# Reordering the first eleven projections behind the join of two transformer blocks, and folding two norms into one token factor

## The reference, cut to what matters

```python
# end of first_block
x = x + swiglu_ffn(rms_norm(x, norm_ffn), w_gate_up, w_down)
x = rms_norm(x, final_norm)                  # norm 2 of the kernel
# start of second_block
x = x + ab_mixer(rms_norm_2(x, ab_norm), ab_w_in, ...)   # norm 3 of the kernel

def ab_mixer(h, ...):
    p = h @ w_in
    qk, va, oa, gates, uv = split(p)         # 1024, 512, 512, 16, 1024 columns
    qk = silu(centred_dwconv(qk, conv_w))    # 5 taps along the tokens
    ...                                      # mLSTM over q, k, va with the gates
    u, vb = split(gelu(uv))
    vb = rms_norm_2(vb by groups)            # then mixed over the tokens by ws
    return concatenate([ha * sigmoid(oa), u * sp]) @ w_out
```

## Time and profile before

| | us |
|---|---|
| median of 3 runs | 895.58 |
| lowest and highest run | 895.4, 896.25 |
| the profiled execution, its own time | 894.72 |
| its span, first to last instruction | 893.0 |
| TensorE busy | 866.3 |
| VectorE busy | 529.4 |
| ScalarE busy | 431.3 |

### The profile page before, as it was taken

How to read it: one execution, slowest core, us unless ns; L and a number is a source line. 1 busy time by engine, 2 the same in 40 slices (tenths; PEclk the granted TensorE clock), 3 DMA queues, 4 the chain that set the end, 5 groups by cost and what they waited for, 6 DMA issues and landing times.

```text
span 893.0 us, 14170 instructions
## 1 busy us (share of the span) xinstructions
PE 866.3 (97%) x5809; PEld 782.9 (88%) x5809; DVE 529.4 (59%) x558; ACT 431.3 (48%) x574; POOL 46.9 (5%) x104
## 2 busy tenths in 40 slices
PE   4999999999999799999999999999999999999997
PEld 4987899999999699888999999989967899999996
DVE  5656554544544669588665555557676765555553
ACT  6366353443444457752654444436565374444441
POOL 4000000000000200211000000003000000000000
PEclk9999999999999899999999999999999999999999
DMA  9821245555546564335675555443611566555511
GB/s 312 302 95 56 86 164 194 185 188 188 188 146 233 185 194 142 142 95 189 184 250 185 186 185 190 142 159 104 216 48 48 189 226 200 187 188 188 188 47 48
DMA packets 98538, 148.20 MB, mean 166 GB/s; under 512 B 4019, under 2 KB 81907, under 8 KB 98499
## 3 DMA queue, kind: packets, MB, share of 16 engines
q1 hardware_dynamic: 97202, 143.11, 48.5%
q0 software_dynamic: 1264, 4.52, 1.7%
q10 hardware_dynamic: 32, 0.02, 0.0%
HBM read 146.57 MB, written 1.05 MB: 165 GB/s over the span
## 4 chain that ended last, share of the span: by engine, by line
PE 93%; DVE 3%; ACT 2%; POOL 1%; DMA 1%; issue 1%; DVEq 0%; POOLq 0%; ACTq 0%
PE bank L1712 28%; PE bank L1713 27%; PE bank L1714 27%; PE bank L1786 1%; PE bank L2285 1%; PE bank L2308 1%; DMA gain<-in_norm_mix 1%; PE bank L2270 1%; PE bank L2264 1%; PE bank L1874 1%; ACT x_norm L646 1%; PE bank L1886 1%; PE bank L1873 1%; PE bank L2039 0%; PE bank L2011 0%
## 5 line engine op out<-in xcount | busy, mean ns | idle before, releaser
L1081 DVE TENSOR_TENSOR w_lo<-w_raw,w_hi 128x2048 fp32r<-128x2048 f32 (+1 forms) x130 | 292.0, 2254 | 151.2 <-ACT w_hi L617 150.9
L1712 PE MATMUL bank<-xT_hi,w_hi 128*128 128x256 f32 x1068 | 304.1, 285 | 0.0
L1714 PE MATMUL bank<-xT_hi,w_lo 128*128 128x256 f32 x1068 | 302.7, 283 | 0.0
L1713 PE MATMUL bank<-xT_lo,w_hi 128*128 128x256 f32 x1068 | 302.7, 283 | 0.0
L617 ACT ACTIVATE w_hi<-w_raw 128x2048 fp32r<-128x2048 f32 (+1 forms) x130 | 243.0, 1878 | 93.2 <-PE bank L1714 83.1
L1712 PEld LDWEIGHTS bank<-xT_hi,w_hi 128*128 128x128 f32 x1068 | 204.3, 191 | 4.2 <-issue 2.4
L1713 PEld LDWEIGHTS bank<-xT_lo,w_hi 128*128 128x128 f32 x1068 | 204.3, 191 | 1.9 <-issue 0.2
L1714 PEld LDWEIGHTS bank<-xT_hi,w_lo 128*128 128x128 f32 x1068 | 204.3, 191 | 0.2
L1712 PE MATMUL bank<-w_hi,ff_hi 128*128 128x512 f32 x344 | 134.6, 391 | 0.0
L1713 PE MATMUL bank<-w_lo,ff_hi 128*128 128x512 f32 x344 | 134.5, 391 | 0.0
L1714 PE MATMUL bank<-w_hi,ff_lo 128*128 128x512 f32 x344 | 134.0, 390 | 0.0
(11 more groups left out here) (234 smaller groups left out, 681.9 us busy)
## 6 DMA issues: line engine op xcount, KB each, us to landing
w_raw<-in_ffn_w SPq DMA_DIRECT2D x64, 1024.0 KB, 5.3
w_raw<-in_ffn_w_gate_up SPq DMA_DIRECT2D x22, 1024.0 KB, 5.1
w_raw<-in_ab_w_in SPq DMA_DIRECT2D x12, 1024.0 KB, 5.3
w_raw<-in_ffn_w_down SPq DMA_DIRECT2D x11, 1024.0 KB, 4.8
w_raw<-in_swa_w_in SPq DMA_DIRECT2D x5, 1024.0 KB, 10.8
w_raw<-in_swa_w_out SPq DMA_DIRECT2D x4, 1024.0 KB, 8.0
w_raw<-in_ab_w_out SPq DMA_DIRECT2D x4, 1024.0 KB, 5.6
w_raw<-in_c_w_out SPq DMA_DIRECT2D x4, 1024.0 KB, 5.2
```

Source lines behind the costliest of these rows:

```text
L1081: dve.tensor_tensor(view(w_lo, ch), view(w_raw, ch), view(w_hi, ch).bitcast(F32), ALU.subtract).then_inc(S["lo_done"], 1)
L1712: pe.matmul(out, sh, mh, start=first, stop=False)
L1713: pe.matmul(out, sh, ml, start=False, stop=False)
L1714: return pe.matmul(out, sl, mh, start=False, stop=last)
```

## The change

- `normalise` no longer runs at the join. VectorE multiplies both gains once (`joined_gains`) and writes `x_norm` = x times both gains (`both_gained`), which is transposed without any token factor. Tile 0's transposes are issued inside the last `down`, tile 1's inside the first visit.
- The raw transposes are split into `uT_hi` and `uT_lo` (`plain_high`, `plain_low`). These two live in `w_hi` and `w_lo` of the slot `up`, which holds no chunk until the seventh of the phase: the ring has three slots until then.
- The two `va` chunks and the two `vb` chunks come first, token-major, with these operands (`plain_visit`). The token factor of both norms together, `ab_rc`, enters as ScalarE's `scale` when the result is read (`mixing_values`, `spatial_values`). The gates come fifth, q and k sixth to ninth, then `u` and `oa` as before.
- For the feature-major chunks the factor must be along the free axis. GpSimd spreads `ab_rc` to 128 columns (`ab_rb`), TensorE transposes it into bank 4, VectorE copies it to `ab_R`, multiplies the transposes in banks 0 to 3 by it in place (`scaled`), and ScalarE and VectorE split that into `xT_hi` and `xT_lo`.
- The second norm's sum of squares is taken over x times the first gain (`first_gained`, `ab_y`); the first token factor is put into `x_res` later by ScalarE, four 128x512 copies with a scale, between the two gelus of `vb`.
- GpSimd makes `ab_r2` and `ab_rc` in small steps, two each token tile; its memsets of the padding wait for the fourth chunk. The gain loads `next_gain(2)` and `next_gain(3)` are behind them.
- VectorE's squares of `vb` and their sum stand before the first `conv` instead of behind the last.
- `decay_rows(0)` waits for the gates' raw row, chunk index 9 for both gelus of `vb`.

```diff
@@ -102,10 +102,12 @@
     add("ffn1", (KT, CW), up)
     add("ffn1", (2, DM), down)
     add("ffn1", (2, DM), spare)
-    cycle[:] = gate, up, down, spare
+    cycle[:] = gate, down, spare, up
     at[0] = 0
     for i in range(13):
-        add("ab_in", (KT, 16 if i == 2 else CW))
+        if i == 3:
+            at[0] += 1
+        add("ab_in", (KT, 16 if i == 4 else CW))
     for _ in range(4):
         add("ab_out", (2, DM))
...
@@ -235,6 +237,25 @@
...
+        uT_hi = w_hi[plain_slot][:].rearrange("p (t k c) -> p t k c", t=NT, k=KT)
+        uT_lo = w_lo[plain_slot][:].rearrange("p (t k c) -> p t k c", t=NT, k=KT)
+        both_gains = take(P, DM)
+        ab_y = take(P, NT, DM)
...
@@ -445,7 +471,8 @@
             uv = 4 * AW + 16
-            at = [i * CW for i in (4, 5)] + [4 * AW] + [i * CW for i in range(4)] + [uv + i * CW for i in (2, 3, 0, 1)] + [3 * AW, 3 * AW + CW]
+            at = ([i * CW for i in (4, 5)] + [uv + i * CW for i in (2, 3)] + [4 * AW] + [i * CW for i in range(4)]
+                  + [uv + i * CW for i in (0, 1)] + [3 * AW, 3 * AW + CW])
...
@@ -547,9 +574,21 @@
-            norm((2, 0), (3, 0), (2, 1), (3, 1))
+            for t in range(NT):
+                pool.wait_ge(S["ssq_ready"], half_turn(2, t, 1))
+                step(pool.tensor_scalar(ab_var[:, t:t + 1], ssq[:, t, 0:1], ssq[:, t, 1:2], EPS, ALU.add, ALU.add))
+                step(pool.tensor_scalar(ab_ev[:, t:t + 1], ab_var[:, t:t + 1], EPS, 0.0, ALU.mult, ALU.add))
+                pool.tensor_tensor(ab_r2[:, t:t + 1], ab_var[:, t:t + 1], minus_half[:, 0:1], ALU.pow).then_inc(S["ab_r2_ready"], 1)
+            for t in range(NT):
+                pool.wait_ge(S["ssq_ready"], half_turn(3, t, 1))
+                step(pool.tensor_scalar(ab_m[:, t:t + 1], ab_ssq[:, t, 0:1], ab_ssq[:, t, 1:2], 0.0, ALU.add, ALU.add))
+                step(pool.tensor_scalar(ab_me[:, t:t + 1], ab_m[:, t:t + 1], ab_ev[:, t:t + 1], 0.0, ALU.add, ALU.add))
+                pool.tensor_tensor(ab_rc[:, t:t + 1], ab_me[:, t:t + 1], minus_half[:, 0:1], ALU.pow).then_inc(S["ab_rc_ready"], 1)
+            pool.wait_ge(S["ab_rc_ready"], NT)
+            pool.tensor_copy(ab_rb, ab_rc.unsqueeze(2).broadcast_to([P, NT, P])).then_inc(S["ab_rb_ready"], 1)
             next_gain(2)
             next_gain(3)
+            pool.wait_ge(S["mm_done"], sched["ab_in"][3].index + 1)
             pool.memset(ab_pad[:, :, 0:2], 0.0)
...
@@ -779,58 +821,89 @@
             split[0] = c[-1].index + 1
-            high_upto(c[-1].index + 1 + 2)
-            sum_squares(2, 0)
-            sum_squares(3, 0)
-            sum_squares(2, 1)
-            transposed_high(2, 0)
-            sum_squares(3, 1)
+            high_upto(c[-1].index + 1 + 1)
             c = sched["ab_in"]
-            high_upto(c[2].index + 1)
-            transposed_high(2, 1)
-            high_upto(c[0].index + SLOTS)
-            for i in range(2):
+            def plain_high(t):
+                for half in range(2):
+                    act.wait_ge(S["t_psum"], 4 * 2 + 2 * t + half + 1)
+                    act.activation(uT_hi[:, t, 4 * half:4 * half + 4, :].rearrange("p k c -> p (k c)"),
+                                   bank[2 * t + half][:], ACT.Copy).then_inc(S["ab_uh"], 1)
+            def scaled_high(t, half):
+                act.wait_ge(S["ab_scaled"], 2 * t + half + 1)
+                act.activation(xT_hi[:, t, 4 * half:4 * half + 4, :].rearrange("p k c -> p (k c)"),
+                               bank[2 * t + half][:], ACT.Copy).then_inc(S["xTh_ready"], 1)
+            def mixing_values(i):
                 ch = c[i]
                 act.wait_ge(S["mm_done"], ch.index + 1)
                 for t in range(NT):
                     last = act.activation(ab_v1[:, t, 2 * i:2 * i + 2, 0:AD],
-                                          bank[AB_BANK[i]][:, t * 256:t * 256 + 256].rearrange("p (a b) -> p a b", a=2), ACT.Copy)
+                                          bank[AB_BANK[i]][:, t * 256:t * 256 + 256].rearrange("p (a b) -> p a b", a=2),
+                                          ACT.Copy, scale=ab_rc[:, t:t + 1])
                 last.then_inc(S["v1_ready"], 1)
-                high_upto(ch.index + 1 + SLOTS)
+            def spatial_values(i):
+                ch = c[2 + i]
+                act.wait_ge(S["mm_done"], ch.index + 1)
+                for t in range(NT):
+                    last = act.activation(ab_vb[:, t, i * CW:(i + 1) * CW], bank[AB_BANK[2 + i]][:, t * CW:(t + 1) * CW],
+                                          ACT.Gelu_apprx_tanh, scale=ab_rc[:, t:t + 1])
+                last.then_inc(S["vb_ready"], 1)
+            plain_high(0)
+            high_upto(c[1].index + 1)
+            sum_squares(2, 0)
+            plain_high(1)
+            high_upto(c[2].index + 1)
+            sum_squares(2, 1)
+            sum_squares(3, 0)
+            sum_squares(3, 1)
+            high_upto(c[3].index + 1)
+            act.wait_ge(S["ab_rc_ready"], NT)
+            mixing_values(0)
+            mixing_values(1)
+            high_upto(c[5].index + 1)
+            for t in range(NT):
+                for half in range(2):
+                    scaled_high(t, half)
+            spatial_values(0)
+            for t in range(NT):
+                for j in range(2):
+                    act.activation(x_res[:, t, HALF_D[j]], ab_y[:, t, HALF_D[j]], ACT.Copy,
+                                   scale=ab_r2[:, t:t + 1]).then_inc(S["ab_res_ready"], 1)
+            spatial_values(1)
+            high_upto(c[7].index + 1)
             act.wait_ge(S["small_loaded"], 64)
-            act.wait_ge(S["mm_done"], c[2].index + 1)
+            act.wait_ge(S["mm_done"], c[4].index + 1)
             act.activation(g_raw, bank[0][0:16, 0:SEQ], ACT.Identity, bias=gate_b[:]).then_inc(S["g_raw_ready"], 1)
             act.wait_ge(S["g_raw_ready"], 1)
             for k in range(4):
                 act.dma_start(g4[:, k, :], g_raw[4 * k:4 * k + 4, :]).then_inc(S["g4_loaded"], 16)
             act.wait_ge(S["pads_ready"], 1)
             act.wait_ge(S["params_ready"], 1)
-            high_upto(c[2].index + 1 + SLOTS)
...
@@ -1320,20 +1393,66 @@
             c = sched["ab_in"]
-            add_residual(2, 0)
+            def joined_gains():
+                n = 3
+                dve.wait_ge(S["gain_loaded"], 16 * (n + 1))
+                step(dve.tensor_tensor(both_gains, gain[:, 0], gain[:, 1], ALU.mult))
+            def both_gained(t, j):
+                d = HALF_D[j]
+                dve.wait_ge(S["resid_ready"], 4 * additions[2] + 2 * t + j + 1)
+                dve.tensor_tensor(x_norm[:, t, d], x_res[:, t, d], both_gains[:, d], ALU.mult).then_inc(S["xn_ready"], 1)
+            def first_gained(t, j):
+                d = HALF_D[j]
+                dve.tensor_tensor(ab_y[:, t, d], x_res[:, t, d], gain[:, 0, d], ALU.mult).then_inc(S["xn_ready"], 1)
+            def plain_low(t):
+                for half in range(2):
+                    dve.wait_ge(S["ab_uh"], 2 * t + half + 1)
+                    k = slice(4 * half, 4 * half + 4)
+                    dve.tensor_tensor(uT_lo[:, t, k, :].rearrange("p k c -> p (k c)"), bank[2 * t + half][:],
+                                      uT_hi[:, t, k, :].rearrange("p k c -> p (k c)").bitcast(F32),
+                                      ALU.subtract).then_inc(S["ab_ul"], 1)
+            def scaled(t, half):
+                b = bank[2 * t + half][:].rearrange("p (k c) -> p k c", c=P)
+                R = ab_R[:, t * P:(t + 1) * P].unsqueeze(1).broadcast_to([P, 4, P])
+                dve.tensor_tensor(b, b, R, ALU.mult).then_inc(S["ab_scaled"], 1)
+            low_upto(c[0].index + 1)
+            joined_gains()
+            for j in range(2):
+                add_residual(2, 0, (j,))
+                both_gained(0, j)
+            plain_low(0)
+            for j in range(2):
+                add_residual(2, 1, (j,))
+                both_gained(1, j)
+            plain_low(1)
             low_upto(c[1].index + 1)
-            normalise(2, 0, x_res)
-            add_residual(2, 1)
-            normalise(3, 0, x_norm)
-            normalise(2, 1, x_res)
-            transposed_low(2, 0)
-            normalise(3, 1, x_norm)
-            low_upto(c[2].index + 1)
+            for t in range(NT):
+                first_gained(t, 0)
+                first_gained(t, 1)
+            low_upto(c[4].index + 1)
+            dve.wait_ge(S["ab_R_psum"], 1)
+            dve.tensor_copy(ab_R, bank[4][:, 0:SEQ]).then_inc(S["ab_R_ready"], 1)
+            dve.wait_ge(S["ab_R_ready"], 1)
+            scaled(0, 0)
+            scaled(0, 1)
+            transposed_low(2, 0, (0,))
+            scaled(1, 0)
+            transposed_low(2, 0, (1,))
+            scaled(1, 1)
             transposed_low(2, 1)
-            low_upto(c[0].index + SLOTS)
             dve.wait_ge(S["params_ready"], 1)
-            for ch in c[0:3]:
-                low_upto(ch.index + 1 + SLOTS)
```

(83 more changed lines are left out.)

36 lines of the change are left out of this document (21 added, 15 removed).

## The result

The changed kernel takes 905.19 us (median of 4 runs, 904.61 to 906.12) against 895.49 for the kernel before on the same chip (4 runs, 894.84 to 896.25). The ratio is 1.0109, 95% interval 1.0091 to 1.0126: slower by 9.7 us where +5.5 was forecast, and 1.3 us above the range. The profiled execution took 904.61, its span is 902.9. The mean granted clock was 0.992 in it and in the execution of 904.62, and 0.989 in the two that took 905.76 and 906.12.

The account below looks back on a forecast made before the run. TensorE, busy 866.3 of 893.0 us, bounds the kernel. 5.8 us won up to the ninth chunk, then waits of 7.1 and 4.3, give +5.5 at `scores_T(0)`: 895.58 + 5.5 = 901.1 us, range 897.4 to 903.9.

Parts of the forecast that it names:

- The join: Between last `down` and `ab_in`: idle and half clock cost 8.2 us; 5.8 won up to the ninth chunk's end.
- Rival D: Join not freed: transposes inside `down` wait longer than 1.1 us and the clock falls there; 904, chance 0.04.
- The factor's readiness: GpSimd's chain to `ab_rc` and `ab_rb`: some 2.3 us and a copy, to about 313; R wanted at 314.9.
- VectorE's wait for the sixth chunk's `high`: Ahead of `xT_lo`: VectorE has scaled half 0 by 317.0, then waits 3.5 us for ScalarE.
- The scalings: VectorE's products in PSUM for the scaled operand: taken at the add's 0.61 to 0.66 us.
- ScalarE's queue: ScalarE from 323.5 to the end of chunk 8's `high` at 337.8: 14.2 us in sum.
- The load: Gelu table load in ScalarE's queue: 1.28 us by the trace, without the skill's added drain of about 1.38.
- The `vb` sums: Squares and their sum on VectorE ahead of `low` 8 and the first `conv` at 340.1: 2.45 us.
- The gate: TensorE's `g_cols` transposes behind the ninth chunk wait 7.1 us for gate rows, from 350.1 to 357.1.
- The clock: The 7.1 us idling lowers the clock, costing some 2.7 us inside `decay_rows(1)`'s 4.3 us wait; nothing added.
- rival C: Clock stays low beyond chunk 9, or falls again in the second wait and slows chunk 10: 903.8, chance 0.17.

Follow-up runs that it names:

- e7: Changed kernel with the old order of chunks, so only the two `va` chunks use the plain operands: 900.27 us, ratio 1.0045.
- e3: Changed kernel with VectorE held until GpSimd has made both token factors, ahead of the `low` of chunks 2 and 3: 907.17 us, a single run.
- e10: Changed kernel with the factor's two transposes one half visit later, behind the third chunk's second token tile: 902.39 us, ratio 1.0082.
- e5: Changed kernel with ScalarE's four `x_res` copies moved from between the two gelus to behind its last pad copy: 903.41 us, ratio 1.009.
- e4: Changed kernel with the `vb` squares and their sum back behind the last `conv`: 904.82 us, ratio 1.011.
- e9: Changed kernel with 24 products that nobody reads between the two decay rows: 904.07 us, ratio 1.0097.
- e6: Changed kernel with `g_cols`, decay rows, `x_res` copies and `vb` sums all later, and the gates' four DMAs issued by GpSimd: 896.12 us, ratio 1.0005.
- e2: Changed kernel with the `g_cols` transposes behind chunk index 9 and both decay rows behind chunk index 10: 899.84 us, ratio 1.0052.

## Why the prediction was right in kind and wrong in size

- *The join.* Right: no low clock at 298 to 310, the tile-0 transposes wait 0.6 (0.2 + 0.9 forecast), the second chunk 0.2 (0.5), `xT_lo` 0.7 (0.6). Rival D falls, and e7 shows that with two plain chunks the waiting only moves to the scaled operand. But 3.5 us are won up to the end of the ninth chunk and not 5.8 (next step).
- *The factor's readiness: the step that failed first, and the larger part of the miss.* The step said that GpSimd's chain takes "some 2.3" us and that, with a copy behind it, the factor is there at "about 313; R is wanted at 314.9", and it booked no wait. The factor was ready at 315.3 (316.2 less 0.9), and the transposes also wait for ScalarE to have emptied bank 4 with the same factor, which the step left out. Measured: 1.1 us of wait and 0.4 of transposes (0.2 booked). The third chunk ends at 319.7 instead of 318.0, and that 1.7, of which 1.3 is these two, is carried unchanged to the first `conv`, 341.9 for 340.1. e3 shows what made the steps slow, e10 that this place was worth 1.5.
- *VectorE's wait for the sixth chunk's `high`*: 3.04 for 3.5. Right, and it is why the transposes could be moved at no cost. The scalings took 0.65 each, as chosen.
- *ScalarE's queue*: 14.2 us forecast from `xT_hi` to the end of the `high`, 14.4 measured (326.17 to 340.5). Right; e5 confirms that it sets the place of the first `conv`. The load cost its 1.28, with the gelu directly behind it, as the row before had shown.
- *The `vb` sums, 2.45 on the path*: wrong as a term. They lie in VectorE's wait for ScalarE (e4), and they left the sum right by luck, because the `high` ended at about the same time.
- *The gate*: 6.8 for 7.1, right as a wait; but both its ends came late, the ninth chunk by 2.2 (352.3 net for 350.1) and the gate rows by 1.9 (359.0 net for 357.1), so that the error of the factor does not show in it.
- *The clock: the other step that failed.* "That costs some 2.7 us, but inside the 4.3 us of wait, so nothing is added." The first fall did lie inside (the decay row's wait shrank to 1.5), but behind the short wait that was left there was a second one, which nothing covers: 1.4 us on chunk index 10. This is the second form of rival C, which I had at 0.17 and at 2.7 us. e9 fills the wait, and in its profile the fall is gone.

The sum: forecast +5.5 at the scores, measured +8.9, the difference being 1.8 to 1.9 for the factor and 1.4 to 1.6 for the second fall. The other 0.8 between +8.9 and the medians' +9.7 lies within the runs' spread and is not attributed; the lower mean clock of two of the four executions (0.989) says that in these the clock was low for longer, but no trace shows where.

What stays open is why the clock sometimes stays high behind a wait of 2.4 us and sometimes not, and why it fell in e6 with no such wait.

## What to carry to other kernels

When a chunk order is changed, follow each small chain that hangs on a chunk (here the gates, from the third place to the fifth) to the place where the bounding engine uses it, and move the use with it; e2 gives back about 5 us so. Price an idle gap of the array by what runs behind it, not by its own length alone: here 1.5 us of waiting was followed by 1.4 us of slow products. Small GpSimd steps beside a large VectorE operation with two SBUF operands should be priced from a row where both were busy.
